# Expert down weights moved from SyncE's DMA queue to ScalarE's, behind the copy of a block's result

## The reference

```
hb = silu(xb @ w_gate[e]) * (xb @ w_up[e])
y  = (hb @ w_down[e]) * wr[:, None]
```

## Time and profile before

| what | value |
|---|---|
| median of 3 runs | 1519.92 us (1519.23 to 1521.69) |
| profiled execution, time and span | 1520.04 us, 1518.3 us |
| PE busy, share of the span | 1324.1 us, 87% |
| expert blocks, first gate/up matmul to the last down matmul | 1009 to 1484 us |
| waits of the down matmuls for down weights | 22.8 us in 19 waits |
| moved by the DMA engines in most of the expert phase | 427 to 430 GB/s |

### The profile page before, as it was taken

One profiled execution on the slowest core, in us unless ns is written; L12 is line 12 of the kernel. 1 busy time (PEld: TensorE's weight loads), 2 busy tenths in 40 slices (PEclk: granted clock), 3 DMA queues, 4 the chain that ended last, 5 costly groups with the idle time before them and its releaser, 6 DMA issues. The chain is left out here.

```text
span 1518.3 us, 19514 instructions
## 1 busy us (share of the span) xinstructions
PE 1324.1 (87%) x6133; PEld 792.5 (52%) x6133; DVE 490.4 (32%) x1080; ACT 244.0 (16%) x644; POOL 206.5 (14%) x401
## 2 busy tenths in 40 slices
PE   5899999999995898877899999669999989899990
PEld 3666667666763455554566664444444443434440
DVE  2236564555456474333000001342122121211123
ACT  1132233223322343222000000000000000000001
POOL 3033442244224111010000000000000000000003
PEclk9799999899997898999899999689999999999995
DMA  6033324332422227553965360259999999999974
GB/s 194 19 111 104 96 83 142 102 98 83 142 59 57 47 50 259 180 149 92 253 139 137 87 217 0 109 232 427 428 430 428 428 428 429 428 429 428 429 303 128
DMA packets 171554, 318.30 MB, mean 210 GB/s; under 512 B 21147, under 2 KB 148563, under 8 KB 159235
## 3 DMA queue, kind: packets, MB, share of 16 engines
q1 hardware_dynamic: 162610, 302.03, 55.0%
q10 hardware_dynamic: 6864, 8.94, 1.7%
q0 software_dynamic: 2048, 6.95, 1.7%
HBM read 289.20 MB, written 28.68 MB: 209 GB/s over the span
## 5 line engine op out<-in xcount | busy, mean ns | idle before, releaser
L670 PE MATMUL psg<-stretch 128*128 128x336 f32 x512 | 159.4, 476 | 11.3 <-DVE h_sample_out L648 9.6
L1734 PE MATMUL ph<-w_gate_up,x_gathered 128*64 128x512 f32 x704 | 162.4, 612 | 0.6 <-DVE x_gathered L1673 0.6
L670 PEld LDWEIGHTS psg<-stretch 128*128 128x128 f32 x512 | 103.6, 204 | 69.0 <-DVE h_sample_out L648 15.4
L1751 PE MATMUL py<-w_down,h_t 128*64 128x512 f32 x512 | 118.5, 605 | 22.8 <-DMA w_down<-in_w_exp_down 22.8
L1685 DVE SCALAR_TENSOR_TENSOR h_gate<-h_tanh,ph 128x256 f32<-128x256 f32 x32 | 13.5, 421 | 344.7 <-ACT h_tanh L1642 344.7
L1734 PEld LDWEIGHTS ph<-w_gate_up,x_gathered 128*64 128x64 f32 x704 | 52.0, 135 | 105.8 <-issue 105.8
L1709 PE MATMUL px<-chunk_rows,yT 128*128 128x192 f32 x516 | 97.9, 332 | 0.0
L1709 PEld LDWEIGHTS px<-chunk_rows,yT 128*128 128x128 f32 x516 | 82.6, 190 | 27.3 <-issue 27.3
L585 DVE SCALAR_TENSOR_TENSOR x_conv<-x_padded,conv_wh,x_conv 128x360 f32<-128x360 f32 x96 | 57.0, 594 | 100.5 <-ACT x_conv L534 89.6
L679 PE MATMUL psg<-stretch 128*128 128x256 f32 (+1 forms) x384 | 84.5, 380 | 0.0
L1347 PE MATMUL psm<-stretch,w_merge 128*128 128x336 f32 x256 | 76.0, 456 | 7.0 <-DMA w_merge<-in_w_in 7.0
(11 more groups left out here) (413 smaller groups left out, 1755.8 us busy)
## 6 DMA issues: line engine op xcount, KB each, us to landing
w_down<-in_w_exp_down SPq DMA_DIRECT2D x32, 2048.0 KB, 25.8
w_gate_up<-in_w_exp_gate SPq DMA_DIRECT2D x22, 2048.0 KB, 22.7
w_gate_up<-in_w_exp_up SPq DMA_DIRECT2D x22, 2048.0 KB, 27.4
stretch<-in_w_exp_gate SPq DMA_DIRECT2D x10, 2048.0 KB, 23.4
stretch<-in_w_exp_up SPq DMA_DIRECT2D x10, 2048.0 KB, 28.0
stretch<-in_w_in SPq DMA_DIRECT2D x16, 1024.0 KB, 5.3
stretch<-in_w_in SPq DMA_DIRECT2D x16, 512.0 KB, 7.6
h<-in_state_ssm SPq DMA_DIRECT2D x16, 512.0 KB, 4.8
```

The lines of the kernel that those rows point to most:

```text
L670: mm = pe.matmul(ps[m][:, 0:T], wg[:, k, P * m:P * m + P], S["xnT"][:, k, :], start=(k == 0), stop=(k == KT - 1))
L1734: mm = pe.matmul(ph[64 * j:64 * j + 64, :], xg[u // 3][:, k, BLK * (u % 3):BLK * (u % 3) + BLK], w_gu[w][:, :, k, :].rearrange("p g (f t) ...
L1751: mm = pe.matmul(py[h][64 * j:64 * j + 64, :], ht[:, k % 2, k // 2, :], w_dn[h][:, k, 512 * j:512 * j + 512], start=(k == 0), stop=(k == 3))
```

## The change

SP no longer issues the down weights. ACT does, for block b+2, after it has issued the two result copies of block b. The wait on `y_ev` goes away, since ACT itself has made the copy that the wait was for. Gate and up stay with SP, with their wait on `gu_free`. Buffers, sizes, matmuls and semaphores of landing are as before.

```
-                with sp.If(b < nblk):
-                    e = sp.value_load(S["blk_e"][0:1, bass.ds(b, 1)], min_val=0, max_val=NE - 1)
-                    sp.wait_ge(y_ev, b + 1)
-                    load_down(sp, A, S, h % 2, e, dn_in[h % 2])
                 with sp.If(b + 2 < nblk):
                     e = sp.value_load(S["blk_e"][0:1, bass.ds(b + 2, 1)], min_val=0, max_val=NE - 1)
                     sp.wait_ge(gu_free, b)
...
                         for j in range(2):
                             act.dma_start(ydram[bass.ds(BLK * b, BLK), j, :], yr[h][64 * j:64 * j + 64, :]
                                           ).then_inc(y_sent[h], 16)
+                    with act.If(b + 2 < nblk):
+                        e = act.value_load(S["blk_e"][0:1, bass.ds(b + 2, 1)], min_val=0, max_val=NE - 1)
+                        load_down(act, A, S, h, e, dn_in[h])
```

## The result

The changed kernel took 1526.62 us (median of 6 runs, 1525.97 to 1528.97) against 1519.59 us for the kernel before (6 runs, 1516.85 to 1521.69): a ratio of 1.0056, interval 1.0041 to 1.0071. It is slower by some 7 us; 1527.9 was predicted. Its profiled execution took 1526.33 us with a span of 1524.7, against 1520.04 and 1518.3 before.

A forecast was written before the change was run, and what follows sets the result against it. PE was taken as the bound at first, the DMA engines from block 11. Lag of 5.4 us there, rising to 9.5, less 1.5 given back, adds 8.0 to 1520.04: 1528.0 (1527.9 against the median); range 1520.5 to 1532.0.

The forecast's parts named there:

- What the change removes and adds: SP's dropped issue and wait gain nothing; ACT issues down weights 2.4 us later, and the tanh is not late.
- The turns: DMA queues alternate packets, not bytes; ACT's needs 19 turns a block, SP's 18, costing 0.55 us: period 15.84 us.
- Step 1: At block 2's down weights: they land at about 1037 us, a lead of 10.7 us before use.
- step 2: Early expert blocks: lead shrinks 1.78 us a block, first wait in block 8, lag about 5.4 us by block 11.
- Step 3: By about block 19 SP's queue runs dry; the lag stops at 9.5 us and the period returns to 15.29.
- Step 4: Last blocks: after SP's last pair ACT's queue has the engines alone, giving back 1.5 us.
- the sum: Over the expert blocks: 9.5 us of lag less 1.5 given back is 8.0 us, for 1528.0 us.
- What would show it: Signs in the profile: up lands in 16 or 17 us, results about 18, down-weight waits about 31 us.
- B: Rival in the expert blocks: waits move from down to gate/up weights, +1.4 us, 1521.3 us; chance 0.18.
- C: Rival in the weight loading: two deep queues move bytes sooner, down waits go, 1516.8 us; chance 0.06.
- D: Rival on ACT: down issue waits for result service, tanh late, 60 us at most, 1540 us taken; chance 0.08.

The follow-up runs named there:

- e1: The changed kernel with each gate and up copy cut into two of 1 MB: 1528.13 us against 1520.11 before, ratio 1.0066.
- e3: The changed kernel with the result copies issued by GpSimd on its own queue instead of by ACT: 1525.89 us against 1520.11 before, ratio 1.0046.
- e4: The changed kernel with each down-weight copy cut into two of 1 MB: 1527.79 us against 1520.11 before, ratio 1.0062.
- e9: The changed kernel with its new condition inside the old one, one branch per empty block: 1523.26 us against 1518.88 before, ratio 1.0045.
- e6: The kernel before, with SP issuing all weights in order of use from block 12 on: 1516.59 us against 1518.65 before, ratio 0.9983.
- e8: The kernel before, all weights on SP's queue, with each gate and up copy cut into two of 1 MB: 1523.93 us against 1518.65, ratio 1.0041.

## Why the prediction was right

**What the change removes and adds.** Right. SP was not late. ACT's issue comes 2.1 us later (2.4 predicted): in block 0, branches and the read of the number take 0.95 us between the result's issue and the down copy's, where 0.7 and an estimated 0.4 made 1.1. The tanh didn't move, and by e1 the delay isn't what costs.

**The turns.** Right, and shown. Before, the weights landed in the order of issue, 5 us apart: gate and up of gu(3), issued at 1017.48 and 1017.93 us, at 1026.0 and 1031.0, d(2), issued at 1024.32, at 1036.2. One copy of 2 MB is 144 packets, 9 per engine: q1 lost 4320 of its 162610 packets for the 30 copies that moved. In the block of rows 6, 384 of the 592 packets are of 8 KB or more and 80 under 512 B, 16 for each of its five copies. The small ones come last: for y(31), which had the engines alone, each copy's 16 passed at the end, some 0.3 us before its landing.

In eight of the blocks that wait, 303 to 305 packets of q1 pass beside 303 to 305 of q10, and the period is 15.9 us (15.84 predicted). That turns are shared out and not bytes shows here between two queues with large packets; from 1117.67 to 1133.56 us:

```profile
q1 hardware_dynamic: 303, 4.44, 65.4%
q10 hardware_dynamic: 304, 2.36, 35.3%
```

The two shares of the 16 engines' time add up to 100.7%, at 428 GB/s: both queues run on the same engines, and the rate is that of before. e1 and e3 change the number of turns on one side and the wait moves to the other; e4 adds turns and the wait comes sooner. The time of the blocks grew by 6.3 us at the same rate, by 5.0 without the clock's fall.

**Step 1 and step 2, the first wait.** It came in block 7, at 1117.67 us, not in block 8 at 1133. The lead that I put at 10.7 us was 9.9: d(2) landed at 1035.7 us and was used at 1045.5. (The 2 us that I gave a copy to start were an estimate; in the trace of before y(31), two copies of 128 KB with the engines to themselves, landed after 2.3 us, of which the bytes take 0.3 at 428 GB/s. But gu(3) was through at 1031.0 us there, not at 1029; from 1018 to 1021 us the engines moved 213 to 344 GB/s.) It then shrank faster than by 1.78 us a block, since the next two down copies landed 16.6 and 18.2 us behind one another before the 15.5 to 15.9 us of the later ones set in. By block 10 the lag was 7.3 us where I had 5.4. The size was off by one block of 1.8 us, the mechanism was right.

**Step 3, the cap, is the step that failed.** I took the point at which SP runs dry for a level at which the lag stays. It is a turning point. Once SP's queue runs empty ACT's has the engines alone (346 packets to 284), the down weights get a lead back, and PE runs at 14.0 us a block until that lead is spent. The clock isn't the cause: the second round, blocks 16 to 26, went the same way with PEclk at 1.00. The lag peaks at 8.5 and 9.3 us, near the 9.5 that I worked out, and falls back to 4.9 and 4.3. Over a whole round, from block 13 at 1211.32 to block 24 at 1380.28 us, a block takes 15.36 us, the 15.29 of one block's bytes and little more. So, by this account, the loss in the end depends on where in the round the last block comes; no run moved the last block within the round.

**Step 4, the end gives back.** Right, but hidden by the clock, of which I had said that it plays no part. From block 27 on the lag rises again, from 4.3 to 5.9 us at block 29. The down weights of block 30 landed at 1463.1 us, before they were needed, as step 4 has it; without the clock's fall block 30 would have followed block 29 after 14.2 us, the lag would have come down to 5.0 us, and the 0.9 us would have been given back. That is an estimate from the 15.51 us measured. The 8.0 us of the sum meet 6.3 in the blocks, of which the turns make 5.0.

**What the sum lacked.** The empty blocks. I counted ACT's new instructions only in blocks where they have cover, and not the ten numbers without a block, where ACT's run to its end is on the path: +1.84 us, of which e9 takes back 1.6. So 5.0 us of turns, 1.3 of the clock and 1.8 of empty blocks make 8.1 in the profiled executions, and 7.0 is the difference of the medians; that both lie near the 8.0 of the sum is in part luck, a loss put too high and two terms left out.

**What would show it.** Up weights landed in 19.7 us, not 16 to 17; results in 11.9 us, not 18: 13 to 15 us in most waiting blocks, where the down copy ahead of them had been issued some 14 us before, and 9.5 to 13.8 in the blocks without a wait. The waits for down weights came to 26.5 us, not 31.

**The rivals.** B (waits move to gate and up, +1.4 us) is what happens when ACT's queue needs few turns: e3 with +0.7 and e1 with +1.5 us beyond its cut. The changed kernel is on the other side of that point by one turn in 19. C fell: no rate above 429 to 430 GB/s in a waiting block. D fell: the tanh was not late.

**Small slips.** The slices at 9 begin with the 28th, not the 27th. From the end of the result copy (1024.15 us) to 1027.2 ACT's work fills 3.05 us, not 3.3. The 0.99 of the granted clock holds one stretch at 0.50, from 1405 to 1408 us. Only this last one bears on the result.

## What to carry to other kernels

Where two deep queues share the DMA engines, count the packets of each per step of work; here the queue with more packets fell behind, though it carried half the bytes (304 packets and 2.36 MB a block against 288 and 4.19 MB), and what is needed first should not stand in such a queue. Where the bytes set the time, the order of the loads still counts, and the order of use was the best of those tried (e6, −3.2 us in the blocks), by little. When code is added to an engine's loop, look at its last rounds too, where it does no work and something may wait for it to finish. And look at what follows a long wait: here some were followed by matmuls at the lower clock (5.00 us instead of 3.65), and behind the last wait nothing made that good.

## What was not expected of the hardware

- One for one held exactly (304 and 304 or 305 packets in one block), although q10's 2.36 MB mix 16 KB packets with small ones and q1's 4.44 to 4.47 MB are nearly all large ones.
- Copies of 1 MB instead of 2 MB moved 424 to 425 GB/s here instead of 429, also with a single queue (e8): 3.9 us of 471.
- An empty round on ACT cost about 0.27 us with one condition (nine steps from 1486.0 to 1488.4 us) and about 0.42 us with two (nine steps from 1490.3 to 1494.1).
- The granted clock fell to 0.50 in some of PE's waits of 2.1 us (blocks 8, 11 and 29) and not in others as long (blocks 17 and 20, 2.06 and 2.10 us); after the last one it cost 1.3 us.
- Two queues nearly equal in turns, 19 and 18 a block, did not settle into an even flow here, but alternated: six and eight blocks with waits, three without behind each.
